# Attention stage of a decoder kernel: finer signals, another order of copies, and an output projection woven between row transposes

## What is computed

```
def memory_cross_attention(x, mem_k, mem_v, w_q, w_o):
    q = (x @ w_q).reshape(B, T, X_HEADS, X_HEAD_DIM)            # 4 heads of 256
    s = jnp.einsum('bthd,bmhd->bhtm', q, mem_k).astype(F32) * (X_HEAD_DIM ** -0.5)
    p = jax.nn.softmax(s, axis=-1).astype(x.dtype)
    o = jnp.einsum('bhtm,bmhd->bthd', p, mem_v).reshape(B, T, D_MODEL)
    return o @ w_o
x = post_norm(x, memory_cross_attention(x, mem_ks[l], mem_vs[l], w_q, w_o), ...)
```

## Time and profile before

| | |
|---|---|
| median of 3 runs | 1459.6 us (1458.09 to 1459.87) |
| profiled execution, its own time | 1458.91 us |
| its span | 1457.2 us |
| mean granted PE clock | 0.987 |
| PE busy, DVE busy, ACT busy | 94%, 71%, 51% |
| attention stage of layer 0 | begins at 358.97 us |
| attention stage of layer 1 | begins at 1008.33 us (1.58 us before 1009.91) |

### The profile page before, as it was taken

How to read it: one execution, slowest core, us unless ns; L and a number is a source line. 1 busy time by engine, 2 the same in 40 slices (tenths; PEclk the granted TensorE clock), 3 DMA queues, 4 the chain that set the end, 5 groups by cost and what they waited for, 6 DMA issues and landing times.

```text
span 1457.2 us, 19818 instructions
## 1 busy us (share of the span) xinstructions
PE 1374.1 (94%) x7772; PEld 1145.4 (79%) x7772; DVE 1034.4 (71%) x1121; ACT 749.1 (51%) x764; POOL 121.2 (8%) x195
## 2 busy tenths in 40 slices
PE   6999999999889999999998999999889999999993
PEld 5879898779767788888886988679767788888882
DVE  4444776683548889898987555781658989898985
ACT  4344643333433777676773532331424776676761
POOL 6000045400000000000000023100000000000000
PEclk9999999999999999999999999999999999999997
DMA  8774454434873699888882354445872799898961
GB/s 245 258 238 148 146 189 123 142 108 181 341 310 116 257 335 335 327 338 321 340 319 97 103 185 165 150 151 201 322 286 87 297 326 343 328 331 332 334 246 37
DMA packets 99682, 343.71 MB, mean 236 GB/s; under 512 B 5968, under 2 KB 32096, under 8 KB 70416
## 3 DMA queue, kind: packets, MB, share of 16 engines
q1 hardware_dynamic: 96048, 330.59, 63.1%
q0 software_dynamic: 3552, 11.99, 2.6%
HBM read 327.61 MB, written 14.94 MB: 235 GB/s over the span
## 4 chain that ended last, share of the span: by engine, by line
PE 81%; DVE 11%; ACT 4%; issue 1%; DMA 1%; POOL 0%; SPq 0%; DVEq 0%; ACTq 0%
PE ps L1668 63%; PE ps L1981 2%; PE ps L2126 2%; DVE x L1149 1%; DVE x L1146 1%; DVE stats L1125 1%; PE ps L2168 1%; PE ps L1751 1%; PE ps L2003 1%; PE ps L2038 1%; DVE mix_s L1391 1%; PE ps L1677 1%; PE ps L1991 1%; PE ps L2068 1%; PE ps L1676 1%
## 5 line engine op out<-in xcount | busy, mean ns | idle before, releaser
L1668 PE MATMUL ps<-w_hi,xt_hi 128*128 128x512 f32 x704 | 280.6, 399 | 13.5 <-DVE w_lo L1088 7.7
L1668 PE MATMUL ps<-w_hi,xt_lo 128*128 128x512 f32 x704 | 276.7, 393 | 0.0
L1088 DVE TENSOR_TENSOR w_lo<-raw,w_hi 128x2048 fp32r<-128x2048 f32 x68 | 155.4, 2294 | 158.6 <-ACT w_hi L732 158.6
L1668 PE MATMUL ps<-w_lo,xt_hi 128*128 128x512 f32 x640 | 251.6, 393 | 0.0
L732 ACT ACTIVATE w_hi<-raw 128x2048 fp32r<-128x2048 f32 x68 | 129.3, 1913 | 175.2 <-PE ps L1668 88.0
L1092 DVE TENSOR_TENSOR moe_lo<-moe_in_raw,w_hi 128x2048 fp32r<-128x2048 f32 x72 | 164.3, 2290 | 30.2 <-ACT w_hi L739 30.1
L1092 DVE TENSOR_TENSOR w_lo<-raw,w_hi 128x2048 fp32r<-128x2048 f32 x72 | 164.9, 2292 | 27.4 <-ACT w_hi L739 26.9
L1668 PEld LDWEIGHTS ps<-w_hi,xt_hi 128*128 128x128 f32 x704 | 133.3, 189 | 44.6 <-issue 8.5
L739 ACT ACTIVATE w_hi<-moe_in_raw 128x2048 fp32r<-128x2048 f32 x72 | 138.4, 1922 | 50.4 <-PE ps L1668 50.4
L1668 PEld LDWEIGHTS ps<-w_hi,xt_lo 128*128 128x128 f32 x704 | 133.0, 189 | 29.7
L739 ACT ACTIVATE w_hi<-raw 128x2048 fp32r<-128x2048 f32 x72 | 137.4, 1911 | 12.6 <-PE ps L1668 12.6
(11 more groups left out here) (369 smaller groups left out, 2370.8 us busy)
## 6 DMA issues: line engine op xcount, KB each, us to landing
raw<-in_moe_w_gate SPq DMA_DIRECT2D x48, 1024.0 KB, 4.9
moe_in_raw<-in_moe_w_down SPq DMA_DIRECT2D x48, 1024.0 KB, 4.9
moe_in_raw<-in_moe_w_up SPq DMA_DIRECT2D x32, 1024.0 KB, 4.9
raw<-in_moe_w_up SPq DMA_DIRECT2D x32, 1024.0 KB, 4.9
raw<-in_xattn_w_kv SPq DMA_DIRECT2D x16, 1024.0 KB, 5.9
raw<-in_hgrn_w_in SPq DMA_DIRECT2D x16, 1024.0 KB, 5.6
raw<-in_cache_mem_k SPq DMA_DIRECT2D x16, 1024.0 KB, 5.0
moe_in_raw<-in_moe_w_gate SPq DMA_DIRECT2D x16, 1024.0 KB, 4.9
```

Source lines behind the costliest of these rows:

```text
L1088: nc.vector.tensor_tensor(lo_at(slot_of(k)), raw_at(slot_of(k)), hi_at(hi_slot(k)).bitcast(F32), ALU.subtract).then_inc(w_low, 1)
L1668: ins = mm(out, lhs, rhs, start=start and n == 0, stop=stop and n == 2, skip_group_check=shared)
```

## The change

Four things. (1) PE waits only for the first query block to be read before it transposes keys, and for the second inside `prompt_scores`, which signals `at_sc` after each token tile (so `at_sc` counts 4 a layer, and all waits on it are renumbered). (2) ACT and DVE do more key copies ahead: ACT copies batch 3 before the second `exps`, DVE copies batch 2 before the second `row_max` and batches 3 and 4 one place earlier against `normalise`; the last `row_max` goes behind the two probability copies. (3) `sample_values(1)` follows `sample_values(0)` directly; `samples_rows(1)` uses banks 6 and 7. (4) The first projection block is no longer `dense` but written out by token tile with `samples_rows(1)` inside it; on ACT and DVE `rows_back(0)` moves behind the first weight split and `rows_out(1)`.

```
--- before.py
+++ after.py
@@ -440,14 +440,14 @@
                             values(l, 1)
                             values(l, 2)
                         elif (kind, n) == ("v", 4):
-                            sp.wait_ge(at_sc, 3 * l + 2)
+                            sp.wait_ge(at_sc, 4 * l + 3)
                             values(l, 5)
                     else:
                         k2 = k - l * KV_CHUNKS - (KV_CHUNKS if n >= KV_CHUNKS else 0)
                         w, col = block_source(k2 // 2)
                         load(k, groups, chunk_of(w, col, k2 % 2))
                         if n == KV_CHUNKS + 1:
-                            sp.wait_ge(at_sc, 3 * l + 3)
+                            sp.wait_ge(at_sc, 4 * l + 4)
                             for n in range(6, BATCHES):
                                 values(l, n)
 
@@ -934,7 +934,7 @@
                     for s in (0, 2):
                         act.wait_ge(at_tr, 4 * (BATCHES * l + n) + s + 1)
                         if n >= KT_SLOTS:
-                            act.wait_ge(at_sc, 3 * l + (1 if n == KT_SLOTS else 2))
+                            act.wait_ge(at_sc, 4 * l + (2 if n == KT_SLOTS else 3))
                         nc.scalar.activation(t_["kt"][:, n % KT_SLOTS, 2 * s:2 * s + 2, :], ps[:, key_bank(n, s), :].rearrange("p (b m) -> p b m", b=2),
                                              ACT.Copy).then_inc(at_ka, 1)
 
@@ -967,15 +967,16 @@
                 def rows_back(r):
                     act.wait_ge(at_ot, 2 * l + r + 1)
                     nc.scalar.activation(xt_hi[:, :, PROMPT + 32 * r:PROMPT + 32 * r + 32].rearrange("p k (b i) -> p k b i", b=4),
-                                         ps[:, 2 - 2 * r:4 - 2 * r, :].rearrange("p a (k b i) -> p (a k) b i", k=4, b=4)[:, :, :, 0:8],
+                                         ps[:, 2 + 4 * r:4 + 4 * r, :].rearrange("p a (k b i) -> p (a k) b i", k=4, b=4)[:, :, :, 0:8],
                                          ACT.Copy).then_inc(at_oh, 1)
 
                 keys_out(0)
                 keys_out(1)
                 exps(0, 4)
                 keys_out(2)
+                keys_out(3)
                 exps(1, 6)
-                for n in range(3, 7):
+                for n in range(4, 7):
                     keys_out(n)
                 exps(2, 2)
                 keys_out(7)
@@ -990,11 +991,11 @@
                                          ACT.Copy).then_inc(at_oh, 1)
                 samples_pt(1)
                 rows_out(0)
-                rows_back(0)
                 splits[0] = chunk_no(db + 4)
                 split(splits[0], groups)
                 splits[0] += 1
                 rows_out(1)
+                rows_back(0)
                 rows_back(1)
                 split(splits[0], groups)
                 splits[0] += 1
@@ -1424,12 +1425,12 @@
                     for s in (1, 3):
                         dve.wait_ge(at_tr, 4 * (BATCHES * l + n) + s + 1)
                         if n >= KT_SLOTS:
-                            dve.wait_ge(at_sc, 3 * l + (1 if n == KT_SLOTS else 2))
+                            dve.wait_ge(at_sc, 4 * l + (2 if n == KT_SLOTS else 3))
                         nc.vector.tensor_copy(t_["kt"][:, n % KT_SLOTS, 2 * s:2 * s + 2, :],
                                               ps[:, key_bank(n, s), :].rearrange("p (b m) -> p b m", b=2)).then_inc(at_kv, 1)
 
                 def row_max(t, banks, scored):
-                    dve.wait_ge(at_sc, 3 * l + scored)
+                    dve.wait_ge(at_sc, 4 * l + scored)
                     s = ps[:, banks:banks + 2, :].rearrange("p a (b m) -> p (a b) m", b=2)
                     link(nc.vector.tensor_reduce(t_["rs"][:, t, :], s, AX_X, ALU.max))
                     nc.vector.tensor_scalar(t_["mx"][:, t, :], t_["rs"][:, t, :], -float(D // XH) ** -0.5, None, ALU.mult).then_inc(at_max, 1)
@@ -1459,7 +1460,7 @@
                 def rows_back(r):
                     dve.wait_ge(at_oh, 4 * l + 2 + r + 1)
                     cols = slice(PROMPT + 32 * r, PROMPT + 32 * r + 32)
-                    bank = ps[:, 2 - 2 * r:4 - 2 * r, :].rearrange("p a (k b i) -> p (a k) b i", k=4, b=4)[:, :, :, 0:8]
+                    bank = ps[:, 2 + 4 * r:4 + 4 * r, :].rearrange("p a (k b i) -> p (a k) b i", k=4, b=4)[:, :, :, 0:8]
                     high = xt_hi[:, :, cols].rearrange("p k (b i) -> p k b i", b=4).bitcast(F32)
                     nc.vector.tensor_tensor(xt_lo[:, :, cols].rearrange("p k (b i) -> p k b i", b=4), bank, high, ALU.subtract)
                     nc.vector.tensor_tensor(xt_hi[:, :, NT + 32 * r:NT + 32 * r + 32].rearrange("p k (b i) -> p k b i", b=4), bank, high, ALU.subtract).then_inc(at_ol, 1)
@@ -1467,21 +1468,21 @@
                 keys_out(0)
                 keys_out(1)
                 row_max(0, 4, 1)
-                row_max(1, 6, 1)
                 keys_out(2)
+                row_max(1, 6, 2)
+                keys_out(3)
                 normalise(0)
-                keys_out(3)
+                keys_out(4)
                 normalise(1)
-                keys_out(4)
                 keys_out(5)
-                row_max(2, 2, 2)
+                row_max(2, 2, 3)
                 keys_out(6)
                 keys_out(7)
                 normalise(2)
                 keys_out(8)
-                row_max(3, 4, 3)
                 prompt_pt(1)
                 prompt_pt(3)
+                row_max(3, 4, 4)
                 samples_pt(0)
                 normalise(3)
                 for c in range(2):
@@ -1961,8 +1962,7 @@
                 block_norm(db + 1, groups, 3 * l, 2 + 3 * l)
                 dense(db + 2, groups, "T")
                 dense(db + 3, groups, "T")
-                for d in (db + 2, db + 3):
-                    pe.wait_ge(evac[d % 2], d // 2 + 1)
+                pe.wait_ge(evac[db % 2], db // 2 + 2)
 
                 t_ = st_att
 
@@ -1983,6 +1983,7 @@
                         ins.then_inc(at_tr, 1)
 
                 def prompt_scores():
+                    pe.wait_ge(evac[(db + 3) % 2], (db + 3) // 2 + 1)
                     pe.wait_ge(at_ka, key_copies(l, 0, 3))
                     pe.wait_ge(at_kv, key_copies(l, 0, 3))
                     for t in range(2):
@@ -1990,7 +1991,7 @@
                             for kc in range(2):
                                 ins = mm(ps[:, 4 + 2 * t + hh // 2, (hh % 2) * MEM:(hh % 2 + 1) * MEM], t_["q"][:, 2 * hh + kc, t * P:(t + 1) * P],
                                          t_["kt"][:, 0, 2 * hh + kc, :], start=kc == 0, stop=kc == 1)
-                    ins.then_inc(at_sc, 1)
+                        ins.then_inc(at_sc, 1)
 
                 def sample_scores(r):
                     pe.wait_ge(at_ka, key_copies(l, 4 * r + 4, 3))
@@ -2046,9 +2047,10 @@
 
                     pe.wait_ge(at_ona, 2 * l + r + 1)
                     pe.wait_ge(at_onv, 2 * l + r + 1)
-                    pe.wait_ge(at_ol, 4 * l + r + 1)
+                    if r == 0:
+                        pe.wait_ge(at_ol, 4 * l + 1)
                     for b8 in range(8):
-                        ins = nc.tensor.transpose(ps[:, 2 - 2 * r + b8 // 4, (b8 % 4) * P:(b8 % 4 + 1) * P], t_["rows"][:, r, b8 * P:(b8 + 1) * P], ident[:])
+                        ins = nc.tensor.transpose(ps[:, 2 + 4 * r + b8 // 4, (b8 % 4) * P:(b8 % 4 + 1) * P], t_["rows"][:, r, b8 * P:(b8 + 1) * P], ident[:])
                     ins.then_inc(at_ot, 1)
 
                 pe.wait_ge(at_ka, key_copies(l, BATCHES - 1, 3))
@@ -2071,11 +2073,26 @@
                 pe.wait_ge(at_p, 4 * l + 4)
                 prob_transposes(3, (4, 5))
                 sample_values(0)
+                sample_values(1)
                 samples_rows(0)
-                sample_values(1)
+
+                def out_half(half, t):
+
+                    k = chunk_no(db + 4) + half
+                    pe.wait_ge(w_low, at(k + 1, groups, GCH))
+                    for kc in range(4):
+                        ins = tile_products(db % 2, slot_of(k), hi_slot(k), kc, 4 * half + kc, t)
+                    if t == 2:
+                        ins.then_inc(w_used, 1)
+
+                pe.wait_ge(at_ol, 4 * l + 2)
+                out_half(0, 0)
                 samples_rows(1)
+                out_half(0, 1)
                 pe.wait_ge(at_ol, 4 * (l + 1))
-                dense(db + 4, groups, "N")
+                out_half(0, 2)
+                for t in range(TILES):
+                    out_half(1, t)
                 block_norm(db + 5, groups, 3 * l + 1, 3 + 3 * l)
 
                 pe.wait_ge(rt_w, 2)
```

## The result

| | before | after |
|---|---|---|
| median, runs on one chip | 1459.45 us (1458.09 to 1459.87, 4 runs) | 1442.54 us (1439.85 to 1444.4, 4 runs) |
| profiled execution, its own time | 1458.91 us | 1439.85 us |
| its span | 1457.2 us | 1438.1 us |
| mean granted PE clock | 0.987 | 0.992 |

The ratio is 0.9884, 95% interval 0.9867 to 0.9902: 16.9 us less, and 1442.0 was forecast. Measured again later, beside nine runs of the kernel before, the changed kernel gave 0.9889 (0.987 to 0.9908).

What follows compares the result with a forecast made beforehand. PE (TensorE) was taken to pace the kernel, with 81% of the chain. Two attention stages, -7.5 in layer 0 and -9.85 in layer 1, took 17.3 off the profiled 1458.9 to 1441.6, median 1442; range 1439 to 1448.5.

Steps and rivals of the forecast that it cites:

- Part A: Attention stage, last query matmul to first sample scores: 19.45 us, -3.85 in layer 0, -4.6 in layer 1.
- Part B: Attention stage, first sample scores to first sample products: PE gains under 0.1 us of a 0.93 gap.
- Part C: Attention stage, first sample products to next block: -3.55 us in layer 0, -5.15 in layer 1 with a clock fall gone.
- rival 2: Second sample products: last value load's landing not moving forward costs 4.2 less 0.5 us per layer, giving 1449.4; chance 0.08.
- The sum: Both attention stages: -7.5 us in layer 0 and -9.85 in layer 1, together -17.3.
- load's ceiling: Value loads: with a DMA ceiling of about 436 GB/s no reordering of loads helps; the trace's 418 was taken to agree.
- The clock: Both attention stages: some 4.9 of the 17.3 us gained comes from falls of PE's granted clock going away.
- Rival 1: Attention stages: the clock still falls, one to four times at 1.6 us, 1443.6 to 1448.4, likeliest 1445; chance 0.2.
- Rival 3: Part A gives only its start, the second maximum and exponentials holding up DVE and ACT: 6 us less, 1448; chance 0.11.
- rival 4: Projection: row transposes between tiles and narrow products in a row take away the full clock; over 1462.5 us; chance 0.02.

Runs made afterwards that it cites:

- combined version: Changed kernel with value loads ahead of output weights, third exponentials and normalising after batch 7 and 8 copies, ACT's first weight split before first row copy: 1439.1 us.
- part C alone: Kernel before with only the two sample products in a row and the projection by token tile between row transposes: ratio 0.9952.
- loads-swapped run: Changed kernel with the value loads of samples 6 to 8 issued before the first two output-weight chunks: ratio 0.9887.
- order-only kernel: Kernel before with only the copies and maxima reordered, signal and waits as before: one run, 1455.44 us.

## Why the prediction was right, step by step

- **Part A** was forecast at 19.45 us and is 19.28, in 14 of 14 stages with all its edits (20.49 and 20.66 with the old start wait). The gap at the start was right (0.25 forecast, 0.22 seen). I worked out 0.7, 0.45 and 0.25 for batches 4 and 5; they are 0.53, 0.42 and none.
- **Which edit wins it.** The prediction gave the later start wait 1.2 us a layer, let the earlier signal close the gap of 2.32, and put no price on the order of the copies. The runs show the signal at 2.6 of the 4.0 us in layer 0, clock included, then the start wait (1.2 to 1.4), then the order (0.2).
- **Part B**: under 0.1 forecast, 0.05 measured. My list of gaps leaves out one of 0.83 us ahead of the second sample scores, where PE waits for ACT's copy of keys. It is 0.83 in all 24 stages of the twelve profiles, the combined version's too, so the sum is unharmed; it is time that no edit here has touched.
- **Part C** was forecast at 24.4 us a layer and is 25.31 and 24.98. The step that was mis-sized is rival 2's: "it is late by 0.2 and hidden by the wait for the split". It is late by 1.0 to 1.3 us, longer than the split's wait of 0.46 and 0.37 that it hides. I read the landing in layer 0 alone (14.3 us after issue), and in that one execution. In layer 0 the same load took 15.1 to 15.4 us in all nine other profiles without swapped loads. And layer 1 of the very profile that I read shows it too; the view of line L428 in the kernel before has its last issue and its longest landing there:

```profile
L428 SPq DMA_DIRECT2D att_kt<-in_cache_mem_v x8: 341/432/1306, 388.2 to 1047.9; - x8
...
DMA to landing us min/median/max: 6.9/11.1/14.9
```

Issued at 1047.9, it landed at 1062.8; the first products end at 1062.28 (the row transposes of layer 1 start at 1063.14, 0.86 later), so the new order would have waited 0.5 us and the 0.14 from a landing to PE. That is close to the 0.64 that part C alone showed in layer 1. With the load out of the way, in the loads-swapped run, part C is 24.47 and 24.44, the forecast to a tenth; the load is the other 0.84 and 0.54 us.
- **The sum** was -17.3 us in two stages and is -16.15. The median moved by 16.9. That it came within 0.5 us of the forecast is in part luck: the stages gave 1.15 us less than forecast, the rest of the kernel gave something that I had put at nothing, and the clock's share rested on which falls one execution happened to have.
- **The reading of the load's ceiling** was wrong in what it left out. I wrote that no reordering of loads helps under a ceiling. A ceiling limits the sum of what is moved; which of five loads lands last is the order's, and the order was worth 0.8 and 0.5 us. The Trainium skill (DMA: Bandwidth & Descriptors, Where 436 GB/s comes from) gives about 436 GB/s for the ports, and puts loads out of HBM at about 358. The trace's 418 GB/s over 3 us is under the first figure and above the second.
- **The clock.** I counted 4.9 of the 17.3 us as clock. In the profiles the gap of 2.32 us had a fall behind it in 5 of 6 stages; the 18 stages without it, where the gaps in the same batches are up to 0.75, had none. The gap alone doesn't decide it: the wait of 1.43 to 1.58 at the start of ten stages had no fall behind it. The projection behind gaps of 1.66 and 1.26 to 1.34 had a fall in 4 of 8 stages (price 1.5 to 1.6 in three of them, 2.8 in the one that lasted longer), and none in 16 stages with both products in a row, though the load wait before it was up to 1.75. So these falls go with the gaps but are not certain: the gain that comes from taking a gap away has a sure part, its length, and a part by chance. The same gap in the order-only kernel gave a fall in one layer and none in the other.
- **Rival 1** (falls stay) did not happen: none in part A in the 16 stages with the earlier signal and the new order together, none at the projection in the 16 with both products in a row. Half the clock for all 64 transposes of batches 2 to 5 would have cost about 7 us a layer, by my estimate from 3.69 us for 32. The combined version ran 48 transposes in 5.50 us, 0.115 each, the same pitch as those 32. The Trainium skill (TensorE: Matmul & The Clock Gate, Part 4) says that the full clock doesn't engage for transposes; the measurement decides against it here. **Rival 3** fell with part A's 19.28, **rival 4** with the clock of 1.00.
- **Outside the stages** I find nothing that the change moved. That no cause but chance moves 1 to 3 us there is argued, not tested by itself. The falls there come and go at the same places whatever the kernel: between 796 and 812 us in seven of the twelve profiles, between 936 and 952 in six, at 12 to 20 in three. And of the 25 runs of the kernel before on one chip, the two slowest (1461.08 and 1461.89 us) had a mean granted clock of 0.983 and the fastest (1453.86) 0.990.

## What to carry to other kernels

When a consumer needs only part of what a run of matmuls makes, signal each part: here one more signal was worth 2.6 us in a stage, and a reordering of the copies 0.2 on top of it and nothing that could be seen without it. Before moving a consumer of a DMA ahead, read that load's landing in every repetition of the stage and allow a microsecond or more (0.2 us late was forecast, 0.64 to 1.75 measured), and put the load that is needed first at the head of a full queue. Where the clock falls behind a gap in one profile, count the gap as gain and the fall as a chance, and compare stage lengths in the traces, since the whole time moved by 8 us (1453.86 to 1461.89 in 25 runs of the kernel before on one chip) with nothing changed.

## What was unexpected of the hardware

The landing of the same load, issued at about the same point of the stage with the loads before it still under way, took 14.1 to 15.4 us over the ten profiles without swapped loads, and 14.3 in the one stage that the prediction read. The wait for it was 0.64 to 1.75 us over twelve stages. In those twelve the landing varies by 0.6 us only (14.8 to 15.4); the rest comes from when the load was issued, since issuing one of the three took anywhere from 0.34 to 1.34 us. And an equal gap of 2.32 us brought the clock to about half in five stages and left it at 1.00 in a sixth; the price of one fall in the projection was 1.5 to 1.6 us in three stages and 2.8 in another, where the clock stayed low for about twice as long.
